# Expert weight loads shared out between two issuing engines: SyncE and ScalarE

## What is computed

```python
def moe_ffn(u, w_router, b_router, w1, b1, w2, b2):
    ...
    top_vals, top_idx = lax.top_k(logits, TOP_K)          # 4 of 32 experts for each token
    gates = jax.nn.softmax(top_vals, axis=-1)
    ...
    def expert_block(args):
        xb, e = args
        hgl = xb @ w1[e] + b1[e]                          # 1024 -> 2048
        glu = jnp.minimum(hgl[:, :D_EXPERT], SWIGLU_LIMIT)
        lin = jnp.clip(hgl[:, D_EXPERT:], -SWIGLU_LIMIT, SWIGLU_LIMIT)
        act = glu * jax.nn.sigmoid(SWIGLU_ALPHA * glu) * (lin + 1.0)
        return act @ w2[e] + b2[e]                        # 1024 -> 1024
    ...
```

## Time and profile before

| | |
|---|---|
| median of 3 runs | 1380.98 us (1380.01 to 1381.06) |
| time of the profiled execution | 1377.24 us |
| its span, first to last instruction | 1375.4 us |
| granted TensorE clock, mean over the span | 0.995 of full speed |
| PE busy / DVE busy / ACT busy | 95% / 31% / 27% of the span |
| bytes moved | 471.33 MB |

### The profile page before, as it was taken

The page is one execution under the profiler, slowest core; times in us unless marked ns, Lnnn a source line. Parts: engine busy times, 40 slices in busy tenths (PEclk is TensorE's granted clock), DMA queues, the critical chain, the costliest instruction groups (busy, mean ns, idle before and its releaser), DMA issues.

```text
span 1375.4 us, 17490 instructions
## 1 busy us (share of the span) xinstructions
PE 1310.5 (95%) x7448; PEld 726.0 (53%) x7448; DVE 427.4 (31%) x810; ACT 364.7 (27%) x558; POOL 34.8 (3%) x57
## 2 busy tenths in 40 slices
PE   6999999999999999999999999999899998899997
PEld 6999999999999433333333333333233333233332
DVE  6765667576553311211111121111121111112111
ACT  5854455654433211111111111111111111111111
POOL 2001200001001000000000000000000000000000
PEclk9999999999999999999999999999999999999999
DMA  7555444359848899999999999999999999999994
GB/s 235 158 152 151 139 143 123 126 183 335 282 148 313 346 402 428 427 428 428 427 427 427 429 426 428 427 428 428 427 427 427 429 428 428 427 427 428 427 429 207
DMA packets 97679, 471.33 MB, mean 343 GB/s; under 512 B 8348, under 2 KB 69928, under 8 KB 71624
## 3 DMA queue, kind: packets, MB, share of 16 engines
q1 hardware_dynamic: 97376, 470.19, 85.2%
q10 hardware_dynamic: 232, 0.07, 0.0%
HBM read 469.19 MB, written 1.05 MB: 342 GB/s over the span
## 4 chain that ended last, share of the span: by engine, by line
PE 67%; DMA 30%; ACT 1%; DVE 1%; issue 0%; DVEq 0%; SPq 0%; ACTq 0%
DMA arena<-in_w_expert_in 30%; PE ps L898 17%; PE ps L925 10%; PE ps L555 7%; PE ps L556 7%; PE ps L557 7%; PE ps L850 3%; PE ps L866 3%; PE ps L546 1%; PE ps L548 1%; PE ps L547 1%; PE ps L858 1%; PE ps L874 1%; PE ps L911 1%; PE ps L907 1%; PE ps L759 1%
## 5 line engine op out<-in xcount | busy, mean ns | idle before, releaser
L898 PE MATMUL ps<-arena 128*64 128x512 f32 x2048 | 455.3, 596 | 43.0 <-DMA arena<-in_w_expert_in 42.6
L898 PEld LDWEIGHTS ps<-arena 128*64 128x64 f32 x2048 | 143.6, 137 | 349.0 <-issue 263.0
L1617 DVE TENSOR_SCALAR arena<-ps 128x512 f32<-128x512 f32 x32 | 22.1, 692 | 683.9 <-PE ps L898 683.9
L925 PE MATMUL ps<-arena 128*64 128x512 f32 x1024 | 226.8, 595 | 0.0
L555 PE MATMUL ps<-A_hi,w_hi 128*128 128x256 f32 x576 | 166.5, 289 | 5.8 <-DVE A_lo L1235 4.5
L556 PE MATMUL ps<-A_lo,w_hi 128*128 128x256 f32 x576 | 163.5, 284 | 0.0
L557 PE MATMUL ps<-A_hi,w_lo 128*128 128x256 f32 x576 | 163.5, 284 | 0.0
L1268 DVE TENSOR_TENSOR w_lo<-w_raw,w_hi 128x1024 fp32r<-128x1024 f32 x120 | 142.7, 1231 | 58.7 <-ACT w_hi L983 58.3
L1199 ACT ACTIVATE arena<-arena 128x512 f32<-128x512 f32 x32 | 20.2, 630 | 460.9 <-DVE arena L1617 460.9
L925 PEld LDWEIGHTS ps<-arena 128*64 128x64 f32 x1024 | 70.7, 137 | 135.7 <-issue 135.7
L983 ACT ACTIVATE w_hi<-w_raw 128x1024 fp32r<-128x1024 f32 x120 | 120.1, 1048 | 24.0 <-DMA w_raw<-in_w_out 7.0
(11 more groups left out here) (305 smaller groups left out, 1342.9 us busy)
## 6 DMA issues: line engine op xcount, KB each, us to landing
arena<-in_w_expert_in SPq DMA_DIRECT2D x120, 2048.0 KB, 45.8
arena<-in_w_expert_out SPq DMA_DIRECT2D x61, 2048.0 KB, 43.6
w_raw<-in_w_in SPq DMA_DIRECT2D x32, 1024.0 KB, 5.5
arena<-in_w_expert_in SPq DMA_DIRECT2D x16, 1024.0 KB, 9.6
w_raw<-in_w_cross_kv SPq DMA_DIRECT2D x8, 1024.0 KB, 7.3
arena<-in_w_expert_out SPq DMA_DIRECT2D x6, 1024.0 KB, 9.2
w_raw<-in_w_ssd_branch SPq DMA_DIRECT2D x4, 1024.0 KB, 5.2
w_raw<-in_w_fox_branch SPq DMA_DIRECT2D x4, 1024.0 KB, 5.2
```

The costliest lines, as they stand in the source:

```text
L898: last = mm(ps[64 * half:64 * (half + 1), b, :], xg_cols[:, 2 * (s % 2) + c, s // 2, :], w[:, at:at + 512], start=False, stop=(s == 3 and ...
L925: last = mm(ps[64 * half:64 * (half + 1), 3, :], at_cols[:, c, s - 4, :], w[:, at:at + 512], start=(s == 4 and c == 0), stop=(s == 5 and c ...
L1617: V_.tensor_scalar(glu, ps[:, 0, :], LIMIT, None, ALU.min).then_inc(glu_ready, 1)
```

## The change

Of the 181 chunks loaded in the expert stage, those with n mod 6 = 4 or 5 are no longer issued by SP. ACT issues them on its own queue, after the copy of `ys` of item i: the pair n = 6i + 4 and 6i + 5, that is chunks 6i + 15 and 6i + 16. These are s3 (the last quarter of the input weights) and s4 (the first half of the output weights) of item i + 2. SP keeps s5, s0, s1 and s2, with its waits as they were. ACT's pair has no wait on `e_used`; ACT has waited for `y_psum >= i + 1` just before. ACT's loop over the first 32 items is written out instruction by instruction, and the loop remains for further items only.

```diff
             for n in range(CHUNKS * NE - SLOTS_W):
-
-                at = n + SLOTS_W
-                sp_.wait_ge(e_used, n + 2)
-                sp_.dma_start(e_slot(at % SLOTS_W), e_chunk(at // CHUNKS, at % CHUNKS)).then_inc(e_loaded[at % SLOTS_W], 16)
+                if n % CHUNKS < 4:
+                    at = n + SLOTS_W
+                    sp_.wait_ge(e_used, n + 2)
+                    sp_.dma_start(e_slot(at % SLOTS_W), e_chunk(at // CHUNKS, at % CHUNKS)).then_inc(e_loaded[at % SLOTS_W], 16)
...
-            with act.Fori(0, n_items) as i:
+
+            def item(i):
                 act.wait_ge(glu_ready, i + 1)
                 A(sig, glu, ACT.Sigmoid, scale=ALPHA).then_inc(sig_ready, 1)
                 gathered_copy(i + 2)
...
                 act.wait_ge(y_psum, i + 1)
                 A(ys, ps[:, 3, :], ACT.Copy).then_inc(y_ready, 1)
+
+            for i in range(NE):
+                item(i)
+                for n in (CHUNKS * i + 4, CHUNKS * i + 5):
+                    at = n + SLOTS_W
+                    if at < CHUNKS * NE:
+                        act.dma_start(e_slot(at % SLOTS_W), e_chunk(at // CHUNKS, at % CHUNKS)).then_inc(e_loaded[at % SLOTS_W], 16)
+            with act.If(n_items > NE):
+                with act.Fori(NE, n_items) as i:
+                    item(i)
```

## The result

The changed kernel takes 1390.08 us (median of 6 runs, 1387.09 to 1390.77) against 1380.49 us beside it: ratio 1.0069, 95% interval 1.0058 to 1.0080. It is slower by 9.6 us. The profiled execution has a span of 1387.8 us for 1375.4, 12.4 more.

What follows compares the result with a forecast made beforehand. DMA transfers at 428 GB/s were taken to bound the expert stage once chunks loaded ahead are used up. 11.2 us for the end (later start included) plus 0.8 for the clock, added to 1380.98, gave 1393.0 us; range 1382 to 1400.

Steps and rivals of the forecast that it cites:

- The bound: Expert stage: PE sets the pace while chunks loaded ahead last, then the DMAs at 428 GB/s, 29.4 us per six chunks.
- the faster rival: Steady phase: two queues move more bytes, up to 2.6%, giving -3 us, 1378 us; decides from 2.0% on; chance 6%.
- Idle time at the start: Start of expert stage: DMA gap grows from 2.1 to 3.7 to 4.2 us, taken as +1.9 us on later landings.
- ACT's time: Two issues behind ACT's copy, 0.7 to 9.4 us, and a possible 1.28 us table load, covered by idle time: 0.
- The order of landing: Steady phase: PE's waits move to s2, alternating between 0 and 5.2 us about a mean of 2.6; nothing lost.
- Equal shares: Both queues, while full, share the DMA engines equally, so ACT's two chunks take 19.6 us; 62%, 1390 to 1396 us.
- The end: Last items: one chunk instead of two lands after s2, so s5 ends 10.4 to 12.0 us later, taken as +11.2.
- Both formulas of the prediction, from 188 and from 182: End of s5: 1376.6 from chunk 188's landing, or 1375.6 + w/2 from chunk 182's, w being that item's s2 wait.
- The clock: After the last long wait the granted clock may fall and slow the matmuls: 0 to +1.7 us, taken as +0.8.
- The order of issue: Rival: chunks issued first move first whatever their queue, so only start idle time counts: +1.9, 1382.9 us; chance 14%.
- the disturbance: Rival: two streams slow each other, 1% less over 590 us is 5.9 us: +18, 1399 us; chance 12%.
- SP first: Rival: ACT's pairs move only when SP's queue is empty, so PE waits for s3 and s4: +31, 1412 us; chance 6%.

Runs made afterwards that it cites:

- experiment 7: Kernel before, with SP's wait for the slot of s5 placed on the end of s5 itself: 1379.16 us, ratio 0.9994, stage 901.6 us.
- experiment 8: Kernel before, with SP's s5-slot wait on the end of s5 and the last s3 (chunk 189) loaded in halves: 1375.33 us, ratio 0.9970.
- experiment 6: The changed kernel with only the first pair (n = 4 and 5) back on SP: 1389.2 us, ratio 1.0066 against the kernel before.
- experiment 3: The changed kernel with only the last pair (chunks 189 and 190) back on SP: 1387.76 us, ratio 1.0064 against the kernel before.
- the second trace of the change: The changed kernel run again from the same file: 1389.62 us, ratio 1.0078 against the kernel before, stage 913.4 us.
- experiment 2: Kernel before, one queue, with only the order of SP's last eight issues changed (189 and 190 ahead of 185 to 188): 1388.66 us, ratio 1.0065.
- experiment 9: The changed kernel with five unread matmuls ahead of the wait for s2 in items 8 to 30: 1391.52 us, ratio 1.0081 against the kernel before.

## Why the prediction was right

*The bound.* Right. The rate of 428 GB/s was a ceiling for two queues as for one; the faster rival needed 2% more and got none. Only "every item of this phase looks like that" was too smooth: of the 19 items from item 13 on, items 16 and 17 have no wait over 0.3 us, and items 18 and 26 wait for s1 as well. The Trainium skill (DMA: Bandwidth & Descriptors, Issuing engines are not separate DMA queues) held too: SP's long issues went away, 328 ns at most each in the change, and nobody had been waiting for them. Before, they took up to 6692 ns over the whole stage; the 4713 that I worked with is the longest of four.

*Idle time at the start.* The gap was right: 1.6 to 2.1 us more forecast, 3.6 - 2.1 = 1.5 more in the windows. That it is paid at the end fits the stage of experiment 7 (1.9 us), and the times of experiment 8 show at least 0.8 us of it; experiment 6, which was to show it on the change itself, doesn't.

*ACT's time.* Right, and with room to spare: 0.35 and 0.45 us a pair, ratio 1.0000 for the written-out program. Had ACT's issues taken as long as SP's longest, 6.69 us, they would have been over the 6.3 us up to which I had called them covered. SP loses 60 issues (30 + 30 now on ACT's queue), not 61.

*The order of landing.* Equal shares were right (13.8 and 24.3 us; my working had 12.5 and 22.3), and so was the place of the waits. They alternate with items without a wait, though not strictly: items 13, 14 and 15 all wait, items 16 to 18 don't. The long ones took 3.0 to 4.7 us, and 6.1 once near the beginning, over the 5.2 that I had as the upper end.

*The end.* The size was right: +11.2 forecast for s5 before the clock, and the stage grew by 9.9 us where chunk 188 set the end and by 12.4, or 10.9 without the slow clock, where the long wait did. The reading behind it was too narrow. I wrote that in the steady phase nothing is lost and the end is where it is lost. The table of starts says otherwise: PE is 11.5 to 16.3 us behind from item 12 on. The DMAs do keep their pace, so the loss doesn't grow, but it is there all along, and repairing the last item's order gives back only what PE can make up in one item. Both formulas of the prediction, from 188 and from 182, were right for the change because the order was wrong up to the last item; used for the last pair alone they gave 2 to 3.6 where 6.7 came out.

*The clock.* The effect is there, where I had 0 to 1.7: behind the wait on which the end hangs it is 1.5 us in one trace of the change and nothing in the other, 2.7 and 2.8 in experiments 3 and 6. That it adds to the end by this much in half of the executions is not shown, and holding the clock up gained nothing.

*The sum.* 1393.0 forecast, 1390.1 measured: +12.0 against +9.6, and the interval ends at +11.0. So the sum was somewhat too high. The profiled execution alone shows +12.4, the second trace of the change a stage longer by 9.9; the runs probably hold both endings, and with them also different starts of the stage. How much each adds to the difference is open. The order of issue, the bytes, the disturbance and SP first are ruled out by the landings, the rate and the place of the waits.

## What to carry to other kernels

Where one stream of loads feeds an engine just in time, a second queue doesn't add bandwidth, it changes the order of landing: what it fetches early delays what is needed next, by as many bytes. Compare when each item starts along the whole stage, and divide what is lost by the slack of the consumer, to see how many items repaying takes. A gap in the transfers at the start of such a stage can come back at the end: here the stages with and without the gap of 2.1 us differed by 1.9 us.

## What was not expected of the hardware

Behind long waits for DMAs in the steady phase the granted clock fell: two microseconds behind the wait that ended at 1271.23 it is at 0.50 (1.2 GHz), and the 32 matmuls took 8.78 us for 7.09.

```profile
1273.00:1275.00 2.00, 2.00 (x8) 0.66 (x6) 0.00 (x0) 0.00 (x0) 0.00 (x0) 0.50 1.00 426
```

Over the waits for s2 in the two traces of the changed kernel and in those with the last one, two or four pairs or the first pair back on SP, this didn't follow the length of the wait alone. Behind waits of 3.9 to 6.1 us the 32 matmuls always took longer, 8.4 to 10.0 us. Behind waits of 3.0 to 3.3 us they took 8.5 to 8.8 us in ten cases and 7.09 in seven. Behind waits of 0.3 to 1.9 us they took 7.09 every time (item 31 of the kernel with four pairs back, where s3 waits as well, left out). Five waits of 1.95 to 1.99 us stand out, with 8.8 us behind each: all five come in the item after one of the seven, as here in items 14 and 15 of the changed kernel.

```profile
856.99 7.09 PE L898 MATMUL ps<-arena 128*64 128x512 f32 x32 [3.17 <-DMA arena<-in_w_expert_in]
...
885.75 8.78 PE L898 MATMUL ps<-arena 128*64 128x512 f32 x32 [1.98 <-DMA arena<-in_w_expert_in]
```

Nor does the clock always fall after the eight matmuls on 32 rows. In ten of the 13 profiled executions the 64 matmuls behind them took 15.2 to 16.8 us; in the other three (experiments 2, 8 and 9) the clock didn't fall there, and experiments 2 and 8 have 13.95 us.
